# Cached keys turned by VectorE in 32x32 blocks instead of by TensorE, in a decoder step on one Trainium2 core

## The reference, cut to what matters

```python
def fox_sample(q, k, v, logf, k_past, v_past, logf_past):
    d_new = lax.cumsum(logf, axis=1).transpose(0, 2, 1)
    rev = (lax.cumsum(logf_past, axis=1, reverse=True) - logf_past).transpose(0, 2, 1)
    sp = jnp.einsum('bqhd,bkhd->bhqk', q, k_past) * scale
    sp = sp + d_new[:, :, :, None] + rev[:, :, None, :]
    sn = jnp.einsum('bqhd,bkhd->bhqk', q, k) * scale
    sn = sn + d_new[:, :, :, None] - d_new[:, :, None, :]
    sn = jnp.where(causal, sn, -jnp.inf)
    p = jax.nn.softmax(jnp.concatenate([sp, sn], axis=-1), axis=-1)
    return p[..., :n_past] @ v_past + p[..., n_past:] @ v

k_past = cache_k[l][page_table].reshape(db, past_len, N_HEADS, HEAD_DIM)
v_past = cache_v[l][page_table].reshape(db, past_len, N_HEADS, HEAD_DIM)
```

## Time and profile before

| | us |
|---|---|
| median of 3 runs | 2178.58 |
| lowest and highest | 2172.83, 2182.11 |
| the profiled execution, first to last instruction | 2187.8 |

### The profile page before, as it was taken

One profiled execution on the slowest core, in us unless ns is written; L12 is line 12 of the kernel. 1 busy time (PEld: TensorE's weight loads), 2 busy tenths in 40 slices (PEclk: granted clock), 3 DMA queues, 4 the chain that ended last, 5 costly groups with the idle time before them and its releaser, 6 DMA issues.

```text
span 2187.8 us, 34891 instructions
## 1 busy us (share of the span) xinstructions
PE 2010.4 (92%) x12990; PEld 1228.5 (56%) x12990; DVE 766.2 (35%) x1789; ACT 491.5 (22%) x1062; POOL 260.7 (12%) x402
## 2 busy tenths in 40 slices
PE   6999998989887999999999989998599999999994
PEld 4677765666654887788887446744333333333331
DVE  5221213555555572333333550623411111111115
ACT  3222222444331010111111021523122222221223
POOL 1101222322231000000000000000011111111110
PEclk9999999999998999999999999999799999999997
DMA  7546777987777022210111120304799999999976
GB/s 273 184 152 224 249 281 244 311 305 266 267 257 246 1 97 79 77 48 10 58 49 70 58 80 1 145 20 173 281 377 383 377 374 371 376 374 374 367 265 243
DMA packets 207153, 458.72 MB, mean 210 GB/s; under 512 B 18753, under 2 KB 48466, under 8 KB 206858
## 3 DMA queue, kind: packets, MB, share of 16 engines
q1 hardware_dynamic: 174410, 357.96, 46.4%
q0 software_dynamic: 32576, 98.53, 13.0%
HBM read 432.51 MB, written 32.17 MB: 212 GB/s over the span
## 4 chain that ended last, share of the span: by engine, by line
PE 82%; DMA 6%; DVE 4%; issue 3%; ACT 2%; SPq 2%; DVEq 1%; ACTq 0%; POOLq 0%
PE ps L1320 16%; PE ps L1625 10%; PE ps L1656 5%; PE ps L1380 5%; PE ps L1636 5%; PE ps L1121 5%; PE ps L1223 5%; PE ps L1409 4%; DMA kraw<-in_cache_k 3%; PE ps L1665 3%; PE ps L1093 3%; PE ps L1136 2%; PE ps L1498 2%; PE ps L1259 2%; PE ps L1234 2%
## 5 line engine op out<-in xcount | busy, mean ns | idle before, releaser
L1625 PE MATMUL ps<-gu,xgT 128*64 128x512 f32 x1024 | 228.5, 599 | 0.9 <-ACT xgT L1989 0.9
L1223 PE MATMUL ps<-consts,kraw 128*128 128x128 f32 x1024 | 141.6, 284 | 32.9 <-DMA kraw<-in_cache_k 27.7
L2985 POOL DMA_DIRECT2D vpage<-in_cache_v x232 | 125.0, 539 | 393.1 <-issue 385.2
L1320 PE MATMUL ps<-xnT,ring 128*128 128x264 f32 x672 | 162.1, 392 | 0.6 <-issue 0.6
L2264 DVE COPY kt<-ps 128x512 f32<-128x512 f32 x128 | 88.4, 691 | 202.6 <-PE ps L1223 201.9
L1223 PEld LDWEIGHTS ps<-consts,kraw 128*128 128x128 f32 x1024 | 116.3, 145 | 61.0 <-DMA kraw<-in_cache_k 30.7
L1625 PEld LDWEIGHTS ps<-gu,xgT 128*64 128x64 f32 x1024 | 71.1, 137 | 133.1 <-issue 130.0
L1320 PEld LDWEIGHTS ps<-xnT,ring 128*128 128x128 f32 x672 | 129.4, 193 | 23.8 <-issue 1.4
L1656 PE MATMUL ps<-wd,hidT_a 128*64 128x512 f32 x512 | 116.9, 598 | 19.6 <-ACT hidT_a L1999 12.7
L2874 DVE TENSOR_TENSOR sig_a<-ps,sig_a 128x256 f32<-128x256 f32 x32 | 13.6, 425 | 325.1 <-ACT sig_a L1993 325.1
L1762 ACT ACTIVATE kt<-ps 128x512 f32<-128x512 f32 x128 | 76.3, 596 | 191.9 <-PE ps L1223 190.0
(11 more groups left out here) (451 smaller groups left out, 3066.1 us busy)
## 6 DMA issues: line engine op xcount, KB each, us to landing
kraw<-in_cache_k SPq DMA_DIRECT2D x256, 256.0 KB, 4.1
gu<-in_w_expert_gate SPq DMA_DIRECT2D x32, 2048.0 KB, 23.4
gu<-in_w_expert_up SPq DMA_DIRECT2D x32, 2048.0 KB, 30.0
wd<-in_w_expert_down SPq DMA_DIRECT2D x31, 2048.0 KB, 8.3
vpage<-in_cache_v POOLq DMA_DIRECT2D x232, 256.0 KB, 4.9
ring<-in_w_in SPq DMA_DIRECT2D x12, 1024.0 KB, 9.1
yy<-y_d SPq DMA_DIRECT2D x16, 512.0 KB, 10.5
early<-in_w_in SPq DMA_DIRECT2D x6, 1024.0 KB, 10.1
```

The lines of the kernel that those rows point to most:

```text
L1223: last = nc.tensor.transpose(bank(R.bank("kt", n, c))[:, j * PAGE:(j + 1) * PAGE], kraw[n % 2][:, j, c * P:(c + 1) * P], ident)
L1320: last = nc.tensor.matmul(bank(R.bank(name, f, q))[:, 0:QT], weight[:, k], src[:, k, cols], start=k == 0, stop=k == HK - 1)
L1625: last = nc.tensor.matmul(bank(0)[h * BA:(h + 1) * BA, :].rearrange("p (x n) -> p x n", x=2), src[:, k, 0:BA], weight[:, k, :, h * DE // 2 ...
L2985: pool.dma_start(vpage[value_place(n)][:, p, :], t["cache_v"][ds(page, 1)].rearrange("a s d -> (a s) d")).then_inc(v_in[value_place(n)], 16)
```

## The change

Keys are loaded in another layout. Page p of a unit goes into partitions 32p to 32p + 31 of `kraw`, four positions of the page (8 KB) to a partition. DVE turns them: one `nc.vector.transpose` turns every 32x32 block in its partition group, and two of them (each 128 partitions x 1024 elements) turn a unit straight from `kraw` into `kt`. PE's 16 transposes of a unit and the copies of turned keys by ACT and DVE are gone. In `kt`, partition group p now holds 32 dimensions of page p. The query operand `qblk` is block-diagonal over the four pages, and the scores again take 16 products of 32 weight columns and 128 moving columns. Rows of the scores are now (head and query, page) with the page varying fastest, so the statistics, `sprobT`, `rev` and the new tokens' scores follow that order. DVE builds `qblk` for each sequence (four small copies). All of the prompt's turned probabilities are now copied by ACT. The load of `nd` moves from SP to POOL. The merging of the softmax parts works on the turned statistics of 8 partitions.

```diff
         def load_keys(eng, n, p, page):
-            eng.dma_start(kraw[n % 2][:, p, :], t["cache_k"][ds(page, 1)].rearrange("a s d -> (a s) d")
+            eng.dma_start(kraw[n % 2][p * 32:(p + 1) * 32], t["cache_k"][ds(page, 1)].rearrange("a (s c) d -> (a s) c d", c=4)
                           ).then_inc(k_in[n % 2], 16)
...
             for n in range(2, NSU):
-                R.made(sp, "kt", n - 2, KC - 1)
+                sp.wait_ge(kt_ready, n - 1)
                 load_unit(n)
...
-                if n == 8:
-                    sp.wait_ge(neg_stored, 16)
-                    sp.dma_start(nd, neg_d[:, SEQ:NT].unsqueeze(1).to_broadcast([H, DS, NS])).then_inc(nd_in, 16)
...
-            def turn_keys(n, some):
-                if n >= NSU:
-                    return
-                pe.wait_ge(k_in[n % 2], 64 * (n // 2 + 1))
-                for c in some:
-                    R.pe_free(pe, "kt", n, c)
-                    for j in range(4):
-                        last = nc.tensor.transpose(bank(R.bank("kt", n, c))[:, j * PAGE:(j + 1) * PAGE],
-                                                   kraw[n % 2][:, j, c * P:(c + 1) * P], ident)
-                    last.then_inc(R.full, 1)
...
             def sample_scores(n):
-                pe.wait_ge(side_ready, Q_READY)
-                R.read(pe, "kt", n, KC - 2), R.read(pe, "kt", n, KC - 1)
+                b = n // SU
+                pe.wait_ge(kt_ready, n + 1)
                 R.pe_free(pe, "sq", n)
-                for c in range(KC):
-                    for j in range(4):
-                        last = nc.tensor.matmul(bank(5)[j * QH:(j + 1) * QH, 0:PAGE], qnew[:, c, n // SU, :],
-                                                kt[n % 2][:, c, j * PAGE:(j + 1) * PAGE], start=c == 0, stop=c == KC - 1)
+                for x in range(4):
+                    first = x // 2 * 16
+                    for j in range(KC):
+                        last = nc.tensor.matmul(bank(5)[j * 32:(j + 1) * 32, 0:PAGE], qblk[b % 2][:, 2 * j + x % 2, first:first + 32],
+                                                kt[n % 2][:, 4 * j + x, :], start=x == 0, stop=x == 3)
                 last.then_inc(R.full, 1)
...
             pe.wait_ge(s_max, DB)
+            pe.wait_ge(side_ready, TOTAL_READY)
             R.pe_free(pe, "turn")
-            nc.tensor.transpose(bank(5)[0:DB, 0:P], negmax, ident).then_inc(R.full, 1)
+            nc.tensor.transpose(bank(5)[0:DB, 0:P], negmax, ident)
+            nc.tensor.transpose(bank(5)[0:DB, P:2 * P], total, ident).then_inc(R.full, 1)
...
+            def spread_queries(b):
+                for g in range(4):
+                    rows = slice(g * 32, (g + 1) * 32)
+                    nc.vector.tensor_copy(
+                        qblk[b % 2].rearrange("p e (x q g) -> p e x q g", x=3, g=4)[rows, :, 0:3:2, :, g],
+                        qgrp[rows, :, :, :, b * DS:(b + 1) * DS].rearrange("p j e x q -> p (j e) x q"))
+                dve.drain()
...
+            for g in range(4):
+                for r in range(4):
+                    nc.vector.tensor_copy(qgrp[g * 32:(g + 1) * 32, :, r % 2, r // 2, :], qs[r * 32:(r + 1) * 32])
+            dve.drain()
+            spread_queries(0)
...
-            def copy_keys(n, c):
+            def turn_keys(n, half):
                 if n >= NSU:
                     return
-                if n >= 2:
-                    R.made(dve, "sq", n - 2)
-                R.made(dve, "kt", n, c)
-                nc.vector.tensor_copy(kt[n % 2][:, c, :], bank(R.bank("kt", n, c))).then_inc(R.by["dve"], 1)
+                if half == 0:
+                    dve.wait_ge(k_in[n % 2], 64 * (n // 2 + 1))
+                    if n >= 2:
+                        R.made(dve, "sq", n - 2)
+                last = nc.vector.transpose(
+                    kt[n % 2].rearrange("p e (s c) -> p c e s", c=4)[:, 2 * half:2 * half + 2],
+                    kraw[n % 2][:, 2 * half:2 * half + 2, :].rearrange("p c (e x) -> p c e x", x=32))
+                if half:
+                    last.then_inc(kt_ready, 1)
...
             for n in range(NSU + LAG):
                 if n < NSU:
                     join_scores(n)
-                copy_keys(n + 2, 1)
+                    if n % SU == 0 and n + SU < NSU:
+                        spread_queries(n // SU + 1)
+                turn_keys(n + 2, 0)
...
                     if x == 0:
-                        copy_keys(n + 2, 3)
-                    copy_turned(k, p)
+                        turn_keys(n + 2, 1)
...
+            dve.wait_ge(s_exp, 3 * DB)
+            nc.vector.tensor_reduce(total, sums, AX, ALU.add).then_inc(side_ready, 1)
...
             pool.dma_start(neg_d, lf[:, 3, :]).then_inc(neg_stored, 16)
+            pool.wait_ge(neg_stored, 16)
+            pool.dma_start(nd, neg_d[:, SEQ:NT].unsqueeze(1).to_broadcast([H, DS, NS])).then_inc(nd_in, 16)
```

More of the change, by code:

```diff
@@ L275, in build_program @@
         pick = at("pick", [P, DB, QH], a_gain + 2048)
-        spread = at("spread", [DB, 4, QH], a_gain + 3072)
+        weighed = at("weighed", [DB, P], a_gain + 2048)
+        parts = at("parts", [DB, P], a_gain + 2560)
+        share = at("share", [DB, P], a_gain + 3072)
         least = at("least", [DB, QH], a_gain + 3584)
@@ L488, in turn_groups @@
             n = UNITS[k][1] + 1
-            return [(g, 4 * g, min(4, n - 4 * g), "act" if (p + g) % 2 == 0 else "dve") for g in range(-(-n // 4))]
+            return [(g, 4 * g, min(4, n - 4 * g)) for g in range(-(-n // 4))]
         END = PROMPT0 + PROMPT_SLOTS
@@ L518, in build_program @@
                 R.add("dve", "po", NU - 1, banks=(4,))
-            for x, (k, p) in enumerate(halves(n)):
+            for k, p in halves(n):
                 if p == 0 and k:
@@ L523, in build_program @@
                     add_scores(k + 1, p)
[L524 to L528, removed]
+                for g, j0, nj in turn_groups(k, p):
+                    R.add("act", "pt", k, p, g, banks=TURNS)
+            for item in items(n):
                 R.add("act", *item, banks=(0, 1, 4))
[L530 to L533, removed]
+            if n == 4:
+                R.add("dve", "snew", banks=TURNS)
             if n == 5:
-                R.add("dve", "snew", banks=TURNS)
+                R.add("dve", "sown", banks=TURNS)
                 R.add("dve", "lf", banks=(0, 1, 4))
@@ L1182, in turn_probs @@
                 pe.wait_ge(f_exp, 2 * k + p + 1)
-                for g, j0, nj, reader in turn_groups(k, p):
+                for g, j0, nj in turn_groups(k, p):
                     R.pe_free(pe, "pt", k, p, g)
@@ L1290, in _ @@
                         prompt_scores(k + 1, p)
-                    if x == 0:
-                        turn_keys(n + 2, (2, 3))
                     turn_probs(k, p)
-                for x, item in enumerate(items(n)):
+                for item in items(n):
                     do_item(*item)
[L1296 to L1299, removed]
+                if n == 4:
+                    new_scores()
                 if n == 5:
-                    new_scores()
+                    spread_new()
                     pe.wait_ge(lf_ready, 1)
@@ L1860, in _ @@
                         exp_prompt(k + 1, 0)
-                for x, item in enumerate(items(n)):
+                for item in items(n):
                     copy_item(*item)
-                    if x == 0:
-                        copy_keys(n + 2, 2)
-                if not halves(n) and not items(n):
-                    copy_keys(n + 2, 2)
                 if KOUT0 <= n < KOUT0 + TILES:
```

160 lines of the change are left out of this document (73 added, 87 removed).

## The result

The changed kernel takes 2267.78 us (median of 4 runs, 2265.35 to 2275.52) against 2178.48 (2172.83 to 2182.11) for the kernel before: a ratio of 1.042, 95% interval 1.039 to 1.045. The forecast was 2160, in a range of 2095 to 2212. The time is 4.2% longer and 56 us above the range. The profiled execution has a span of 2267.5 us, 79.7 more than before's 2187.8, and all of it arises in the loop over cache units. The medians differ by 89.3 us.

The account below looks back on a forecast made before the run. TensorE was taken to bound the loop, fully until 188 us, with late keys as second limit. Terms of -21, -1, -3 and +6 gave -19 us: 2160 us from 2178.6, in a range of 2095 to 2212.

Parts of the forecast that it names:

- What bounds the kernel: Loop over cache units: PE bound up to 188 us; then PE still sets the pace, DMA share 0.76 to 0.81.
- First stretch, -21: Loop, 84 to 188 us: 23.7 us of PE transposes gained, less later start and one more product; net -21 us.
- The cost of narrow keys, 229 GB/s: Key loads into 32 partitions move 229 GB/s, so a unit's keys occupy all engines 4.6 us instead of 3.1.
- 1.5 us of engine time a unit: Loop from 188 us: narrow keys add 1.5 us a unit to today's DMA time; net -1, -3 and +6 us by stretch.
- The turn, 1.23 us: DVE's transpose of 128x1024 in the loop: 1.23 us an instruction, 2.5 us a unit; bounds 0.69 and 2.27.
- No bound yet, even at 2.27 us (219): DVE's load from 356 to 620 us: 153 of 264 us, or 219 with turns of 2.27 us, so no bound.
- The ends: From 620 us on: values only untouched, 0; final merging's wait of some 2 us covered by convolution slack, 0.
- Transfers overlap: Rival, chance 0.18: pages in different partition groups overlap, keys cost no more than today; gain of 90 us, 2088.
- Keys come late: Rival, chance 0.25: landing of 10 to 11 us, slots of 8.9 us against 8.0, granted clock falls; +25 us, 2204.
- The turn costs 2.27: Rival, chance 0.05: DVE's turn takes 2.27 us per instruction, a slot grows by 1.0 us; 2195.
- What would show it: Signs: first stretch some 20 us shorter; later DMA share 0.93 or more, GB/s near 280, landing 6 to 8 us.

Follow-up runs that it names:

- e2_before_narrow: The kernel before, with key pages loaded into 32 partitions (8 KB each) as in the change, still turned by TensorE; 2271.49 us, ratio 1.044 to the kernel before.
- e1_after_wide: The changed kernel with key pages loaded as before into all 128 partitions (2 KB each), VectorE's turns kept; 2158.99 us, ratio 0.990 to the kernel before.
- e5_wide_copy: The changed kernel with full-height key loads and copies in place of VectorE's transposes; 2123.65 us, ratio 0.976 to the kernel before.
- e3_after_order: The changed kernel with a unit's four pages issued in the order 0, 2, 1, 3, alternating partition halves; 2234.14 us, ratio 1.025 to the kernel before.

## Why the prediction was wrong, step by step

- **What bounds the kernel.** Right: TensorE up to 188 us, DMA engines close behind from there.
- **First stretch, -21.** Measured -15.7. The gain of the transposes came. The start is later than assumed: the first joining stands at 90.48 us instead of 84.28, as DVE builds the operands and then turns two units in 7.48 us. I had about 2 us for that, it is 6. The timelines of PE and of DVE in the kernel after:

```profile
86.81 1.94 PE L1222 MATMUL ps<-kt,qblk 128*32 128x128 f32 x32 [15.58 <-DVE kt L2241]
```

```profile
82.97 7.48 DVE L2241 STREAM_TRANSPOSE kt<-kraw 128x1024 f32<-128x1024 f32 x4
```

- **The cost of narrow keys, 229 GB/s.** The mechanism was right, and for keys alone the size was near: with no values beside them the narrow loads cost 1.1 us a unit more (e2_before_narrow, 84 to 188 us), where I had 1.5. With values beside them it was not: SP's queue moved 203 to 226 GB/s, and the key pages in it less by the estimate above.
- **The step that failed: 1.5 us of engine time a unit, added to a share that else stays as it was.** Each stretch's sum took the share of before and added 1.5 us a unit, so it left the value pages at 344 GB/s. They fell to 234 and 280. Measured from unit 12 to 28, the engine time rose by 183 - 114 = 69 us for 16 units, 4.3 a unit; in e2_before_narrow it rose by 2.2 a unit. By the total rates of after, the 45.2 MB that before moved from 188 to 356 us (269 GB/s) need 206 us at 219 GB/s, 38 more; I had 4 less. Units 12 to 28 lost 36.4. The 75 MB that before moved from unit 28 to unit 60 (269 us at 278 GB/s) need 321 us at 233, 52 more; I had 6. These units lost 59.7. The sum then would have been -16 + 38 + 52 = +74, against the 79.7 measured. This takes the mixed rates from the kernel after, so it shows where the time went and not that it could have been forecast. The row that priced the narrow load held both kinds of load one after the other; for the mix I added the two prices, each by its own bytes, and no row showed that they add. They do not; how the loads slow each other inside the engines no run shows.
- **The turn, 1.23 us.** Measured 2.03, inside the bounds given (0.69 to 2.27), and beyond the value taken. In the change it costs some 7 us, within the noise, since the DMA engines set the pace.
- **"No bound yet, even at 2.27 us (219)".** This was wrong in kind, and hidden in the change: DVE was compared by its busy time. With wide loads the turns, instead of copies, cost 31 to 35 us (e1_after_wide to e5_wide_copy) with DVE 73% busy, since DVE waits for the keys ahead of work that PE waits for. I had named DVE's queue ahead of the turn but not what stands behind it.
- **The ends.** Right. From the last unit's scores to the first product of the convolution it is 61.9 us (59.8 before), and from there to the end 1491.8 (1495.1).
- **The rivals.** "Transfers overlap" fell: e3_after_order shows 6%, not a doubling. "Keys come late" had the sign and the fallen clock. Its landing of 10 to 11 us came from 188 to 356 us (median 9.9, worst 22.5) but not from 356 to 620 (7.2), and its slot of 8.9 us was too short. From unit 28 to 60 a slot took 10.3 us (8.4 before, not the 8.0 that I took), since the rival counted the price of lateness alone and not of full engines. Its own sign, a DMA share of 0.85, did not come. "The turn costs 2.27" was nearly true of the instruction and worth little here.
- **What would show it.** DMA share of 0.93 or more: yes. GB/s near 280: no, 233. PE's share of 0.65 (0.66) and a landing of 6 to 8 us (7.2 from 356 to 620 us) came as well, so of the signs for the DMA engines only the GB/s separates the forecast from what happened.

## What to carry to other kernels

When a load is made narrower, price all transfers that share the engines, not the narrow one alone, and measure the mix: a one-line edit of the kernel before, as in e2_before_narrow, would have shown 2271 us at once. Here engines 0.8 busy had no room for it. A layout that wants pages in 32-partition groups can be had from one indirect load over all 128 partitions. Of an engine that gets new work, check the order of its queue, not its share: what stands behind the new wait, and who waits for that.

## What was not expected of the hardware

- Value pages over 128 partitions, on another queue, dropped from 344 to 280 GB/s from 356 to 620 us while narrow loads ran, in both kernels with narrow keys. From 188 to 356 us it was 368 before, 234 in the change and 18.98/(0.390 x 168) = 290 in e2_before_narrow.
- The DVE transpose in 32x32 blocks of 128x1024 float32 takes 2.03 us, the copy between the same tiles 1.10. The Trainium skill, page "Vector Engine (DVE) Microarchitecture Reference", section "3.8 The reshape front-end and per-opcode configuration", has the transposing array sustain one element per cycle and lane. The runs show nearly twice the time of the copy; both had the same access patterns, and whether another pattern suits the transpose better no run here tells.
- A gather of 1 MB in 8 KB rows by one instruction occupied POOL for about 1.0 us, and its queue moved 349 GB/s, no less than plain loads of pages (337 to 339 in e1_after_wide).
